# Two closing units of a transformer block's input projection, computed as three fp32r products of rounded and rest parts

## The reference

```python
u = x * (1.0 + sc1[:, None]) + sh1[:, None]
z = u @ w_in[l]                      # (512, 1024) @ (1024, 3272)
aq, ckv, iq, ik, iw, hq, hf, hi, hg = jnp.split(z, SPLIT_POINTS, axis=-1)
ya = _dsa_attention(aq, _rmsnorm(ckv), iq, ik, iw, w_uk, w_uv, rel_bias)
yb = _hgrn2(hq, hf, hi, hg, lbs[l], gnorm_g[l])
y = jnp.concatenate([ya, yb], axis=-1) @ w_out[l]
```

## Time and profile before

| | us |
|---|---|
| runs | 1223.85, 1224.49, 1232.37 |
| median | 1224.49 |
| profiled execution, its time | 1228.33 |
| profiled execution, its span in the trace | 1226.5 |
| TensorE busy in that span | 1149.4 (94%) |
| VectorE busy | 923.0 (75%) |
| ScalarE busy | 470.4 (38%) |

### The profile page before, as it was taken

How to read it: one execution, slowest core, us unless ns; L and a number is a source line. 1 busy time by engine, 2 the same in 40 slices (tenths; PEclk the granted TensorE clock), 3 DMA queues, 4 the chain that set the end, 5 groups by cost and what they waited for, 6 DMA issues and landing times.

```text
span 1226.5 us, 14606 instructions
## 1 busy us (share of the span) xinstructions
PE 1149.4 (94%) x4720; PEld 753.6 (61%) x4722; DVE 923.0 (75%) x1381; ACT 470.4 (38%) x612; POOL 230.7 (19%) x119
## 2 busy tenths in 40 slices
PE   3799999998798999899999999999999999999966
PEld 3453445665554468677777777777777777777632
DVE  4578975766342668798888888888888888888857
ACT  0213303225562013244444444444444444444421
POOL 0000000000000001022222222222222222222670
PEclk9798999998798989999999999999999999999988
DMA  9991255103502035689999999999999999999793
GB/s 349 368 397 56 79 84 130 46 24 110 200 1 103 30 142 221 250 291 378 392 380 388 375 390 380 381 377 382 379 391 372 379 376 390 366 395 392 271 392 143
DMA packets 77817, 335.68 MB, mean 274 GB/s; under 512 B 14376, under 2 KB 16296, under 8 KB 52824
## 3 DMA queue, kind: packets, MB, share of 16 engines
q1 hardware_dynamic: 58680, 293.15, 63.4%
q0 software_dynamic: 13824, 33.58, 7.4%
q10 hardware_dynamic: 5280, 8.53, 2.0%
HBM read 309.51 MB, written 42.48 MB: 287 GB/s over the span
## 4 chain that ended last, share of the span: by engine, by line
PE 88%; DMA 3%; DVE 3%; POOL 2%; issue 2%; ACT 2%; SPq 1%; ACTq 0%; DVEq 0%; POOLq 0%
PE ps L734 18%; PE ps L761 15%; PE ps L739 14%; PE ps L1488 10%; PE ps L1496 5%; PE ps L1695 5%; PE ps L789 4%; PE ps L1559 2%; PE ps L799 2%; PE ps L855 2%; POOL wx L575 2%; PE ps L1665 2%; PE ps L1516 1%; PE ps L747 1%; PE ps L1646 1%
## 5 line engine op out<-in xcount | busy, mean ns | idle before, releaser
L546 POOL DMA_INDIRECT xg<-u_rows,idx x64 | 182.9, 2858 | 495.5 <-DVE idx L1026 495.2
L734 PE MATMUL ps<-wx,xT 128*128 128x512 f32 x512 | 235.4, 602 | 0.1
L897 DVE TENSOR_TENSOR gu_lo<-wx,gu_hi 128x2048 fp32r<-128x2048 f32 x64 | 146.6, 2291 | 57.0 <-ACT gu_hi L625 57.0
L892 DVE TENSOR_TENSOR wd_lo<-wx,wd_hi 128x2048 fp32r<-128x2048 f32 x65 | 148.5, 2285 | 3.6 <-ACT wd_hi L1446 3.0
L734 PEld LDWEIGHTS ps<-wx,xT 128*128 128x128 f32 x512 | 92.1, 190 | 92.0 <-issue 91.8
L638 ACT ACTIVATE hs<-ps 128x256 f32<-128x256 f32 x68 | 26.1, 384 | 301.9 <-PE ps L739 281.2
L618 ACT ACTIVATE wd_hi<-wx 128x2048 fp32r<-128x2048 f32 x64 | 122.5, 1914 | 26.2 <-PE ps L761 26.2
L739 PE MATMUL ps<-gu_hi,xT_hi 128*128 128x512 f32 x256 | 126.2, 493 | 0.4 <-DVE gu_lo L897 0.4
L625 ACT ACTIVATE gu_hi<-wx 128x2048 fp32r<-128x2048 f32 x64 | 122.2, 1909 | 0.0
L1488 PE MATMUL ps<-uT,ring 128*128 128x512 f32 x272 | 118.8, 596 | 0.0
L761 PE MATMUL ps<-wd_hi,hT_hi 128*128 128x512 f32 x272 | 113.0, 415 | 4.3 <-DVE hT_lo L911 4.3
(11 more groups left out here) (287 smaller groups left out, 1783.7 us busy)
## 6 DMA issues: line engine op xcount, KB each, us to landing
wx<-in_w_gate SPq DMA_DIRECT2D x64, 1024.0 KB, 7.9
wx<-in_w_up SPq DMA_DIRECT2D x64, 1024.0 KB, 11.1
wx<-in_w_down SPq DMA_DIRECT2D x64, 1024.0 KB, 8.9
expert_rows<-yrow SPq DMA_DIRECT2D x64, 512.0 KB, 6.7
ring<-in_w_ada SPq DMA_DIRECT2D x7, 2048.0 KB, 13.9
ring<-in_w_in SPq DMA_DIRECT2D x6, 2048.0 KB, 15.9
vg<-in_w_ada SPq DMA_DIRECT2D x2, 2048.0 KB, 13.0
fk<-in_w_ada SPq DMA_DIRECT2D x2, 2048.0 KB, 14.9
```

Of the source, the lines that this page charges most:

```text
L546: pool.indirect_dma_start(out=xg[:, buf, :], out_offset=None, in_=u2_d[:, :], in_offset=bass.IndirectOffsetOnAxis(ap=idx[:, col:col + 1], ...
L734: pe.matmul(bank, xT_raw[:, j - J3, :], raw[:, :, j, :], start=(j == J3), stop=False)
L892: dve.tensor_tensor(wd_lo[s][:], w, wd_hi[:].bitcast(F32), ALU.subtract).then_inc(wd_ready, 1)
L897: dve.tensor_tensor(gu_lo[s][:, :, 0:J3, :], gate_up_weights(s)[:, :, 0:J3, :], gu_hi[:].bitcast(F32), ALU.subtract).then_inc(gu_lo_ready, 1)
```

## The change

Units Z0 + 5 and Z0 + 6 (tiles n = 4 to 11) are computed by split products. ScalarE makes the rounded parts and VectorE the rests; `uT` is split once into the free ring slots 3 (rounded) and 2 (rest), the weights' rounded parts go into buffers that are idle then (`aqT`, `ybT`, `work`, `prob`, `oT`, `adaacc`), and the rests are written over the weights in their ring slots. Z0 + 6 now goes into slot 0, so its load waits for Z0 + 4; OUT0 goes into slot 3 and OUT0 + 1 into slot 0, and both loads wait for all of z. SyncE's order changes with that.

```diff
+        uT_hi, uT_lo = ring_r[3][:], ring_r[2][:]
+        hi9 = [aqT_hi[:], ybT_hi[:]]
+        hi10 = [work_hi[:], prob_hi[:], oT_hi[:], adaacc_hi[:]]
...
+        SLOT = [0, 1, 2, 3, 0, 1, 2, 3, 0, 1, 0, 3, 0]
+        FREED = [None, None, None, None, 0, 1, 2, 3, 4, 5, 8, 10, 10]
...
@@ SyncE
                 if n >= RING:
-                    unit_free(sp, n - RING)
+                    unit_free(sp, FREED[n])
...
             load_unit(Z0 + 5)
-            load_unit(Z0 + 6)
             sp.wait_ge(vb_ready, 1)
             sp.dma_start(vbias_d, vb.unsqueeze(1).broadcast_to([HA, P, NBIAS])).then_inc(vb_stored, 16)
             sp.wait_ge(mrow_ready, 1)
             sp.dma_start(mods_d, mrow[:, 0, :]).then_inc(mrow_stored, 16)
+            load_unit(Z0 + 6)
+            sp.wait_ge(z_done, sum(z_tiles[:6]))
+            load_rows(6)
             load_unit(OUT0)
             load_unit(OUT0 + 1)
-            sp.wait_ge(z_done, sum(z_tiles[:6]))
-            load_rows(6)
-            sp.wait_ge(z_done, sum(z_tiles))
             load_rows(7)
...
@@ ScalarE, for n, dst in enumerate(rest):
+                if n == 1:
+                    unit_free(act, Z0 + 3)
+                    act.activation(uT_hi, uT[:], ACT.Copy).then_inc(split_hi, 1)
+                    act.wait_ge(mrow_stored, 16)
+                    unit_full(act, Z0 + 5)
+                    for m in range(2):
+                        act.activation(hi9[m], ring[:, SLOT[Z0 + 5], 4 * m:4 * m + 4, :], ACT.Copy).then_inc(split_hi, 1)
+                if 6 <= n < 10:
+                    if n == 6:
+                        unit_full(act, Z0 + 6)
+                        act.wait_ge(vb_stored, 16)
+                    act.activation(hi10[n - 6], ring[:, SLOT[Z0 + 6], :, (n - 6) * P:(n - 5) * P], ACT.Copy).then_inc(split_hi, 1)
...
@@ TensorE
+            def token_tile_split(unit, t):
+
+                bank = z_bank()
+                for j in range(KD):
+                    pe.wait_ge(split_lo, j // 4 + 2)
+                    lo = ring_r[SLOT[unit]][:, j, :]
+                    at = slice(t * P, (t + 1) * P)
+                    for k, (a, w_) in enumerate(((uT_hi, hi9[j // 4][:, j % 4, :]), (uT_hi, lo), (uT_lo, hi9[j // 4][:, j % 4, :]))):
+                        mm = pe.matmul(bank[:], a[:, j, at], w_, start=(j == 0 and k == 0), stop=(j == KD - 1 and k == 2))
+                mm.then_inc(z_done, 1)
+
+            def feature_tile_split(unit, m):
+
+                bank = z_bank()
+                pe.wait_ge(split_lo, m + 4)
+                for j in range(KD):
+                    lo = ring_r[SLOT[unit]][:, j, m * P:(m + 1) * P]
+                    for k, (w_, a) in enumerate(((hi10[m][:, j, :], uT_hi), (lo, uT_hi), (hi10[m][:, j, :], uT_lo))):
+                        mm = pe.matmul(bank[:], w_, a[:, j, :], start=(j == 0 and k == 0), stop=(j == KD - 1 and k == 2))
+                mm.then_inc(z_done, 1)
...
@@ VectorE, behind the scans of L1854 and ahead of kT (L1857)
+            dve.wait_ge(split_hi, 1)
+            unit_free(dve, Z0 + 2)
+            dve.tensor_tensor(uT_lo, uT[:], uT_hi.bitcast(F32), ALU.subtract).then_inc(split_lo, 1)
+            for m_ in range(2):
+                raw = ring[:, SLOT[Z0 + 5], 4 * m_:4 * m_ + 4, :]
+                dve.wait_ge(split_hi, m_ + 2)
+                dve.tensor_tensor(ring_r[SLOT[Z0 + 5]][:, 4 * m_:4 * m_ + 4, :], raw, hi9[m_].bitcast(F32), ALU.subtract).then_inc(split_lo, 1)
...
@@ VectorE, in the loop over LEVELS, behind the products of L1887 and L1888
+                if 2 <= l < 6:
+                    raw = ring[:, SLOT[Z0 + 6], :, (l - 2) * P:(l - 1) * P]
+                    dve.wait_ge(split_hi, l + 2)
+                    dve.tensor_tensor(ring_r[SLOT[Z0 + 6]][:, :, (l - 2) * P:(l - 1) * P], raw, hi10[l - 2].bitcast(F32), ALU.subtract).then_inc(split_lo, 1)
```

More of the change, by code:

```diff
@@ L110, in build @@
             gu_hi = sb("gu_hi", [P, 2, J3, ED], F32R, at=over)
+        with ExitStack() as over:
+            aqT_hi = sb("aqT_hi", [P, 4, W], F32R, at=over)
         aqT = sb("aqT", [P, 4, T])
@@ L121, in build @@
         trunk = ctx.enter_context(ExitStack())
+        with ExitStack() as over:
+            ring_r = [sb(f"ring_r{i}", [P, KD, W], F32R, at=over) for i in range(RING)]
         ring = sb("ring", [P, RING, KD, W], at=trunk)
@@ L127, in build @@
         big2 = sb("big2", [P, 4, 1024], at=trunk)
+        with ExitStack() as over:
+            ybT_hi = sb("ybT_hi", [P, 4, W], F32R, at=over)
         ybT = sb("ybT", [P, 4, T], at=trunk)
@@ L132, in build @@
         selb = sb("selb", [P, 1280], BF16, at=trunk)
+        with ExitStack() as over:
+            work_hi = sb("work_hi", [P, KD, P], F32R, at=over)
         work = sb("work", [P, 2, 512], at=trunk)
+        with ExitStack() as over:
+            prob_hi = sb("prob_hi", [P, KD, P], F32R, at=over)
         prob = sb("prob", [P, 2, 512], at=trunk)
+        with ExitStack() as over:
+            oT_hi = sb("oT_hi", [P, KD, P], F32R, at=over)
         oT = sb("oT", [P, 2, 512], at=trunk)
         ya = sb("ya", [P, 512], at=trunk)
+        with ExitStack() as over:
+            adaacc_hi = sb("adaacc_hi", [P, KD, P], F32R, at=over)
         adaacc = sb("adaacc", [P, 2, W], at=trunk)
@@ L303, in build @@
         units += [("out", [(0, n, W)]) for n in (0, 512)]
+        SLOT = [0, 1, 2, 3, 0, 1, 2, 3, 0, 1, 0, 3, 0]
+        FREED = [None, None, None, None, 0, 1, 2, 3, 4, 5, 8, 10, 10]
         full_at, filled = [], [0] * RING
         for n, (kind, parts) in enumerate(units):
-            filled[n % RING] += 16 * (1 if kind == "ada" else len(parts))
-            full_at.append(filled[n % RING])
+            filled[SLOT[n]] += 16 * (1 if kind == "ada" else len(parts))
+            full_at.append(filled[SLOT[n]])
         z_tiles = [4, 1 + NT, 4, 4, NT, NT, 4]
@@ L316, in unit_full @@
         def unit_full(eng, n):
-            eng.wait_ge(ring_full[n % RING], full_at[n])
+            eng.wait_ge(ring_full[SLOT[n]], full_at[n])
         def unit_free(eng, n):
@@ L330, in build @@
         r_read = sem("r_read")
+        split_hi = sem("split_hi")
+        split_lo = sem("split_lo")
         u2_ready = sem("u2_ready")
@@ L1166, in load_unit @@
                 for at, col, w in parts:
-                    sp.dma_start(ring[:, n % RING, :, at:at + w], src[:, :, col:col + w]).then_inc(ring_full[n % RING], 16)
+                    sp.dma_start(ring[:, SLOT[n], :, at:at + w], src[:, :, col:col + w]).then_inc(ring_full[SLOT[n]], 16)
             def load_rows(k):
@@ L1487, in feature_tile @@
                         pe.wait_ge(ut_ready, j + 1)
-                    mm = pe.matmul(bank[:], ring[:, unit % RING, j, col:col + P], uT[:, j, :],
+                    mm = pe.matmul(bank[:], ring[:, SLOT[unit], j, col:col + P], uT[:, j, :],
                                    start=(j == 0), stop=(j == KD - 1))
@@ L1495, in token_tile @@
                 for j in range(KD):
-                    mm = pe.matmul(bank[:, 0:w], uT[:, j, t * P:(t + 1) * P], ring[:, unit % RING, j, col:col + w],
+                    mm = pe.matmul(bank[:, 0:w], uT[:, j, t * P:(t + 1) * P], ring[:, SLOT[unit], j, col:col + w],
                                    start=(j == 0), stop=(j == KD - 1))
@@ L1561, in level @@
                     mm.then_inc(att_done, 1)
+            def token_tile_split(unit, t):
[15 more added lines that the diff above has]
+                mm.then_inc(z_done, 1)
             for n in range(12):
                 unit, m = Z0 + 4 + n // 4, n % 4
-                if m == 0:
+                if n == 0:
                     unit_full(pe, unit)
-                if n < 8:
+                if n < 4:
                     token_tile(unit, m, 0, W)
+                elif n < 8:
+                    token_tile_split(unit, m)
                 else:
-                    feature_tile(unit, m * P)
+                    feature_tile_split(unit, m)
                 if n == 2:
@@ L1695, in project @@
                         mm = pe.matmul(ps[2 * (t % 2) + half][:], src[:, j % 4, t * P:(t + 1) * P],
-                                       ring[:, (OUT0 + half) % RING, j, :], start=(j == 0), stop=(j == KD - 1))
+                                       ring[:, SLOT[OUT0 + half], j, :], start=(j == 0), stop=(j == KD - 1))
                 mm.then_inc(wo_done, 1)
```

## The result

The changed kernel took 1211.62 us (median of 4 runs, 1209.93 to 1213.29) against 1224.17 for the one before: a ratio of 0.9873 with a 95% interval of 0.9836 to 0.9909. Forecast were 1214.5 in a range of 1210.2 to 1220.5, and 0.77 on a change within 1%. The time lies in the range, but the measured change is 1.3% by this ratio (1.0% by the two medians alone), on the faster side of the 1% to which I had given only 0.20. The profiled execution took 1211.71 us with a span of 1209.9, against 1228.33 and 1226.5: 16.6 us, more than the medians differ in any of the three measurements (12.8 at most). All medians are of fast executions alone; a slow one of 1489.89 us under "Holding the clock" and one of 4083.91 us under "Each unit alone" are left out.

A forecast was written before the change was run, and what follows sets the result against it. TensorE was taken to bound the stretch: eight tiles at 1.25 us each give 10.0 us off with nothing back, so the median goes from 1224.49 to 1214.5 us; range 1210.2 to 1220.5, 8 times in 10.

The forecast's parts named there:

- What bounds the stretch: From 201 to 286 us TensorE is the bound, without an idle bracket; shorter tiles shorten the stretch.
- The tiles: Eight TensorE tiles go from 6.87 to 5.62 us each, 24 products of 0.231 plus 0.08: 10.0 us gained.
- the 0.08 us of each tile's first product: The first product behind the transposes and its waits takes 0.31 us, 0.08 more than the others.
- rival 1: TensorE's fp32r product is as fast as a float32 pass, 0.215 us: 13.7 us off, 1210.8; chance 0.07.
- Cover for the parts: ScalarE's and VectorE's work on parts ahead of tile 4 is all covered, with 6 us left.
- the queue: SyncE's later loads cost nothing: Z0 + 6 lands 7 us early, bands and output weights have 2 to 3 us to spare.
- the end: The pause ahead of L1585 still hangs on the last tile's copy, 0.7 us to spare; the last 1.25 us count too.
- Rivals 2: Each wait costs TensorE 0.08 us, even when long satisfied, in token tiles: 7.8 us off, 1216.7; chance 0.12.
- 3: The loop of VectorE and ScalarE binds at 10.0 us in four periods: 6.8 us off, 1217.7; chance 0.10.
- 4: ScalarE waits ahead of `hi9` for the adaLN rows' store: 14 us lost, 10 gained, 1228.5; chance 0.05.
- the line at 12.2: The 1% of the whole time that a measurement can tell from no change, 12.2 us; 0.77 on staying within it.

The follow-up runs named there:

- three measurements: The changed kernel, unaltered, measured three times against the kernel before: ratios 0.9873, 0.9917 and 0.9897.
- Holding the clock: Changed kernel plus throw-away float32 products in TensorE's pauses around the last transposes and first attention steps: 1211.24 us, ratio 0.9899.
- Each unit alone: Two kernels, each with only one of the change's units split and the other in float32: Z0 + 5 alone 1217.24 us, Z0 + 6 alone 1219.49.
- padded kernel: Changed kernel plus 6 throw-away products ahead of each split tile, so tiles last as long as in float32: 1225.47 us, ratio 1.0017.
- one-wait kernel: Changed kernel with one wait per token tile instead of one ahead of each contraction step: 1211.45 us, ratio 0.9906.
- three rests: Changed kernel plus two more VectorE subtractions of 128x1024 behind each of the four rests in the level loop: 1217.03 us, ratio 0.9935.
- unheld profiles in the table: Five traces without throw-away products, two of the kernel before and three of the changed one; level 0 to transposes 88.59, 88.58 and three times 77.88 us.
- the kernel with the order alone: Changed kernel's slots and SyncE order, but all twelve closing tiles in float32 and no parts made: 1224.69 us, ratio 1.0017 against before.
- held kernels: Kernel before and changed kernel, both with throw-away products in TensorE's earlier and later pauses: 1217.39 us (0.9951) and 1204.63 us (0.9835).

## Why the prediction was right or wrong

**What bounds the stretch: right.** TensorE has no bracket between 197.71 and 270.5 in the profile after, and the padded kernel gave all of the gain back.

**The tiles: right in kind, 0.7 us too small.** Forecast 5.62 us a tile, measured 5.54 and 5.69. The mis-sized term is the 0.08 us of each tile's first product, 8 x 0.08 = 0.64 us in all. That product does take 0.31, but the level ahead of it is then 3.49 rather than 3.57 long, so the 0.08 only moves from one row to the next and costs nothing. It goes with a split tile that follows the level, not with one that came before: level 0, which follows a float32 tile, takes 3.49, and the level from a split tile to a float32 one takes 3.57. The other 0.07 are the products, 0.227 and 0.234 rather than 0.231. By periods 1.41 and 1.27 us were saved instead of 1.25. The 216 ns of the Trainium skill (TensorE: Matmul & The Clock Gate, section Back-to-back issue gap) were not reached; 227 ns is the shortest spacing here. So rival 1 did not come about.

**Cover for the parts, the queue and the end: right.** Rivals 2, 3 and 4 are refuted by the one-wait kernel, by the three rests with their margin of 1 us a round, and by ScalarE's `hi9` at 180.87. The bands and the output weights were in time.

**The sentence that failed** is "The rest of the program hangs on this stretch by one chain and moves with it; short stretches at half the granted clock between 286 and 327 may fall elsewhere, for which I allow 2 us either way". The 2 us were too few. The half clock's stretches reach to 460, not 327 (0.56 over 384 to 388 and 0.55 over 456 to 460 in the very profile that the forecast was made from), and one lies ahead of level 0. From the attention to the projection alone the unheld profiles in the table span 4.95 us (79.18 and 74.23; 3.15 within the kernel before alone), and the start of level 0 another 3.25. Windows of the kernel before and then of the kernel after, over the first attention steps (TensorE busy, granted clock, DMA share, GB/s):

```profile
308.00:312.00 4.00, 2.01 (x10) 0.67 0.70 280
312.00:316.00 4.00, 1.55 (x9) 0.50 0.94 377
316.00:320.00 4.00, 3.66 (x14) 0.50 1.03 421
320.00:324.00 4.00, 4.00 (x17) 0.50 0.80 304
324.00:328.00 4.00, 4.00 (x15) 0.69 0.02 9
```

```profile
296.00:300.00 4.00, 1.70 (x9) 0.66 0.89 314
300.00:304.00 4.00, 2.26 (x11) 0.50 1.03 402
304.00:308.00 4.00, 3.80 (x14) 0.56 1.02 418
308.00:312.00 4.00, 3.30 (x23) 1.00 0.87 309
```

Before, the clock is at half (1.2 GHz) from 312 to 324, with TensorE busy only 2.01 and 1.55 of 4 us in the two windows around its fall; after, it is full again (2.4 GHz) by 308. Of 79.18 - 74.23 = 4.95 us between the two profiles 1.76 are the products of the last adaLN row, at half clock before (3.57 rather than 1.81), and the other 3.19 lie ahead of them, where the half clock lasted longer before. The 16.6 us are then: 0.32 ahead of level 0, 10.71 by the tiles, 0.65 and 4.95 around the attention, 0.22 up to the experts, -0.25 behind. No run shows these parts to be the change's doing, so that the first median came out at 12.55 rather than near 10.7 may be the luck of the executions. The forecast's working ended on the tiles' 10.0 us and drew the line at 12.2; a 1% line 2 us off a forecast with a scatter of this size doesn't leave 0.77 on one side. My reading now would be: 10 to 11 us in the trace, and a median of a few runs that may show 9 to 14, so near 0.6 to 0.4.

**Still open.** Whether the change itself makes the half clock rarer or shorter. Its three differences average 11.9 us, 1.2 above the tiles. The scatter of the medians allows a difference of 1.2 with no cause in the change, and it allows a small gain of another kind: the kernel with the order alone and the padded one lie above before, not below, so such a gain would have to come with the earlier start of what follows. No run tells these apart. Nor is it settled why the held kernels differ by 12.8 us in their medians and by 11.2 in their spans, nor why the throw-away products gave 4.5 us to the kernel before and 7.5 to the changed one.

## What to carry to other kernels

Where TensorE streams float32 without a pause, three fp32r products of parts take 5.5 to 5.7 us for 6.9, provided that VectorE and ScalarE have the room for the parts. Count the margin of the engine that makes them by its whole round, not by its idle time: here 1 us a round was left. Before a forecast of under 1%, take the trace apart at fixed points: the changed stretch is exact to 0.02 us, and what moves beside it, here the stretches at half clock, sets how wide the range of the time must be. Those stretches are themselves worth more than many edits. The best kernel of this study is the changed one with cheap products in TensorE's pauses: 1204.63 us against 1212.15.

## What the hardware showed that I had not expected

- Filling only the first pauses gave nothing in the median (1211.24), filling the later ones too gave 7.5 us (1204.63 against 1212.15). In the trace with the first ones filled the clock fell to half (1.2 GHz) among the last attention steps, where it stayed full in two of the change's three profiles.
- Products of the same shape took 0.227 to 0.229 us in the four token tiles and 0.233 to 0.234 in the four feature tiles. The former load 128 columns of u and stream 512 of the weights, the latter the other way round.
- The issue of the same DMAs on ScalarE's queue took between 1.31 and 3.47 us for three of them, with a copy that the path needs behind it.
- Executions of the kernel before lie between 1219.67 and 1233.77 us on one chip, and two profiles of it 7.8 us apart, with no difference in the stretch from level 0 to the transposes.
